# Two blocks of a network on one core: both FFNs' second products in seven block products instead of eight

## The reference

```python
def conv_ffn(h, p):                       # first block; D_FF = 2816
    a, b = jnp.split(h @ p["ffn_w_up"], 2, axis=-1)
    a = short_conv(a, p["ffn_conv_w"], p["ffn_conv_b"])
    return (jax.nn.gelu(a, approximate=False) * b) @ p["ffn_w_down"]

def conv_glu(x, w_up, conv_w, conv_b, w_down):   # second block
    hid = conv3(x @ w_up) + conv_b        # causal, per feature
    gate, up = hid[..., :D_FF], hid[..., D_FF:]
    return (jax.nn.silu(gate) * up) @ w_down
...
    x = x + g_f * conv_ffn(...)           # first block
    x = x + conv_glu(...)                 # second block
```

## Time and profile before

| | us |
|---|---|
| runs of the kernel, median of 3 (lowest to highest) | 3330.58 (3327.54 to 3332.19) |
| the profiled execution, its own time | 3329.57 |
| its span in the trace | 3327.7 |
| TensorE busy (matmuls) | 3179.3 (96%) |
| VectorE busy | 2189.8 (66%) |
| ScalarE busy | 1247.1 (37%) |
| POOL busy | 858.4 (26%) |
| mean granted clock of TensorE | 0.979 |
| down, first FFN | about 1487.5 to 1729.7 |
| down, second FFN | about 3084.8 to 3324.4 |

### The profile page before, as it was taken

How to read it: one execution, slowest core, us unless ns; L and a number is a source line. 1 busy time by engine, 2 the same in 40 slices (tenths; PEclk the granted TensorE clock), 3 DMA queues, 4 the chain that set the end, 5 groups by cost and what they waited for, 6 DMA issues and landing times.

```text
span 3327.7 us, 37104 instructions
## 1 busy us (share of the span) xinstructions
PE 3179.3 (96%) x14586; PEld 2477.6 (74%) x14586; DVE 2189.8 (66%) x2724; ACT 1247.1 (37%) x1912; POOL 858.4 (26%) x858
## 2 busy tenths in 40 slices
...
GB/s 227 158 136 118 146 202 45 45 9 247 223 145 162 100 84 83 83 124 170 156 120 115 102 127 184 177 107 39 38 72 117 155 83 83 89 83 84 198 133 123
DMA packets 110518, 406.82 MB, mean 122 GB/s; under 512 B 14376, under 2 KB 17000, under 8 KB 105866
## 3 DMA queue, kind: packets, MB, share of 16 engines
...
## 4 chain that ended last, share of the span: by engine, by line
PE 65%; DVE 8%; ACT 2%; issue 2%; POOL 1%; DMA 0%; ACTq 0%; DVEq 0%; POOLq 0%
PE PS L395 20%; PE PS L397 20%; PE PS L396 20%; PE PS L3112 2%; PE PS L3151 2%; PE PS L3134 1%; DVE HL L351 1%; POOL Sc L3360 1%; DVE E L3286 1%; ACT HL L333 0%; PE PS L2774 0%; DVE HT L1903 0%; DVE H L3412 0%; DVE HTf L1786 0%; DVE H L2498 0%
## 5 line engine op out<-in xcount | busy, mean ns | idle before, releaser
L395 PE MATMUL PS<-H,HL 128*128 128x512 f32 x1920 | 759.6, 396 | 15.2 <-DVE H L3412 7.3
L397 PE MATMUL PS<-H,HL 128*128 128x512 f32 x1920 | 751.1, 391 | 0.0
L396 PE MATMUL PS<-H,HL 128*128 128x512 f32 x1920 | 751.0, 391 | 0.0
L351 DVE TENSOR_TENSOR HL<-RAW,HL 128x512 fp32r<-128x512 f32 (+1 forms) x407 | 438.1, 1077 | 414.9 <-ACT HL L333 405.3
L333 ACT ACTIVATE HL<-RAW 128x512 fp32r<-128x512 f32 (+1 forms) x407 | 337.6, 830 | 921.6 <-PE PS L397 859.3
L395 PEld LDWEIGHTS PS<-H,HL 128*128 128x128 f32 x1920 | 362.6, 189 | 104.8 <-issue 19.7
L396 PEld LDWEIGHTS PS<-H,HL 128*128 128x128 f32 x1920 | 362.7, 189 | 76.5 <-issue 2.6
L397 PEld LDWEIGHTS PS<-H,HL 128*128 128x128 f32 x1920 | 362.4, 189 | 76.3
L395 PE MATMUL PS<-HT,HL 128*128 128x512 f32 x720 | 282.6, 393 | 17.8 <-DVE rows L2225 15.7
L396 PE MATMUL PS<-HT,HL 128*128 128x512 f32 x720 | 281.8, 391 | 0.0
L397 PE MATMUL PS<-HT,HL 128*128 128x512 f32 x720 | 281.4, 391 | 0.0
...
## 6 DMA issues: line engine op xcount, KB each, us to landing
RAW<-in_w_up SPq DMA_DIRECT2D x100, 512.0 KB, 3.6
RAW<-in_w_down SPq DMA_DIRECT2D x88, 512.0 KB, 3.6
RAW<-in_w_proj SPq DMA_DIRECT2D x48, 512.0 KB, 3.7
scr_hid<-hidr POOLq DMA_DIRECT2D x36, 512.0 KB, 2.9
...
RAW<-in_w_wmodr SPq DMA_DIRECT2D x32, 512.0 KB, 4.3
HL<-in_w_dfwd POOLq DMA_DIRECT2D x16, 1024.0 KB, 7.1
HL<-in_w_dinv POOLq DMA_DIRECT2D x16, 1024.0 KB, 5.3
```

Of the source, the lines that this page charges most:

```text
L351: e.tensor_tensor(lo, part_source(k, j, x)[0], hi.bitcast(F32), ALU.subtract).then_inc(*k.low.mark(j, x))
L395: e.matmul(out, lh, rh, start=first, stop=False)
L396: e.matmul(out, lh, rl, start=False, stop=False)
L397: return e.matmul(out, ll, rh, start=False, stop=last)
```

## The change

The hidden rows of a *pair* of blocks (2p, 2p+1) and the two halves of the tokens form a 2 x 2 matrix of blocks, and so do the two blocks' weights and the two halves of the 1024 output features. Their product takes seven block products of 128 x 128 x 512 by four banks instead of eight. There are 11 pairs (`PAIRS`; the two kept pairs come first) and seven phases (`PHASES`): m1, m2, m6, m7, m5, m4, m3. All 11 pairs of a phase follow one another, twelve matmuls each: 77 steps.

- The sums of results are not formed on VectorE. A phase goes on adding in the banks that the earlier one used: m1, m6, m5, m3 in banks 0 to 3, m2, m7, m4 in banks 4 to 7 (only m1, m2 and m7 begin anew). After each phase its four banks are added to the quarter of the residual that they then belong to (`ADDED`). Every addition waits for the residual's four loads, as before.
- All 18 stored blocks are loaded once, in twelve larger loads, into room that the up stage has left (`load_place`: `Hf`, `HTf`, `rows`, `cv2`) and stay there. POOL issues them ahead of the residual's loads; those into `rows` and `cv2` wait for the last hidden block.
- VectorE forms the sums of rows in place (`hidden_sum`, 44 an FFN, when: `T_AT`) and the sums of weights eight steps ahead (`weight_sum`): for m6 two operations per pair (out of a "sum" unit and half a "spare" unit in `RAW`), whose result `s2` is kept, and from it m5's and m3's by one each; m7's by one out of a "difference" unit. m1, m2 and m4 use weights as they are.
- Weights are loaded in units of two half blocks ("halves"), and for m6 in 6 spare and 11 sum units, for m7 in 11 difference units. A sum or spare unit's buffer comes free when its sum is done.
- Rows are split four steps ahead, into four places (`hs3` is new), weights six steps ahead by halves.
- The residual's features are complete in another order (`SETTLED`), and the norm between the FFNs follows it; two of its weight units are split earlier, and the last four additions stand behind them.

Core of the diff:

```diff
+PHASES = ["m1", "m2", "m6", "m7", "m5", "m4", "m3"]
+PAIRS = [9, 10] + list(range(9))
+NP = len(PAIRS)
+GROUPS = [[i for i in (g, g + 1) if i < NP] for g in range(0, NP, 2)]
...
-        for _ in range(2):
-            units(down, DOWN)
+        for x in PHASES:
+            for g, steps in enumerate(GROUPS):
+                if x != "m7":
+                    out.append((down, (x, g), "spare" if x == "m6" else "halves"))
+                if x in ("m6", "m7"):
+                    out.extend((down, (x, i), "sum" if x == "m6" else "difference") for i in steps)
...
+def down_source(k, name, i, kind):
+    x, n = i
+    w = k.A["w_" + name]
+    if kind == "difference":
+        return w[2 * PAIRS[n]]
+    if kind == "sum":
+        return w[2 * PAIRS[n]:2 * PAIRS[n] + 2, :, 512:1024].rearrange("t k n -> k t n")
+    p, m = PAIRS[GROUPS[n][0]], len(GROUPS[n])
+    f, h = {"m1": (0, 0), "m2": (1, 0), "m6": (0, 0), "m5": (0, 0), "m4": (1, 1), "m3": (1, 0)}[x]
+    return w.rearrange("(p two) k n -> two k p n", two=2)[f][:, p:p + m, blk(h, 512)]
...
+            elif before in ("halves", "difference"):
+                e.wait_ge(*k.low.at(b, down_parts(k.sched[b][1], before)[-1]))
+            elif before in ("spare", "sum"):
+                x, n = k.sched[b][1]
+                e.wait_ge(*ffn_of(k, b).s.dve.at("ws", 2 * NP + (GROUPS[n][-1] if before == "spare" else n)))
             else:
                 e.wait_ge(*k.low.at(b, "m4"))
-        e.dma_start(k.RAW[:, k.slot[j], :], k.A["w_" + name][i]).then_inc(*k.raw[k.slot[j]].mark(j))
+        if kind in DOWN_KINDS:
+            src = down_source(k, name, i, kind)
+            if kind == "difference":
+                to = k.RAW[:, k.slot[j], :]
+            else:
+                n = 2 if kind == "sum" else len(GROUPS[i[1]])
+                to = k.RAW[:, k.slot[j], 0:512 * n].rearrange("p (t n) -> p t n", t=n)
+        else:
+            src, to = k.A["w_" + name][i], k.RAW[:, k.slot[j], :]
+        e.dma_start(to, src).then_inc(*k.raw[k.slot[j]].mark(j))
...
+N_HS = 4
...
+SUMMED = ("m6", "m7", "m5", "m3")
+ADDED = {"m1": (0, range(0, 4)), "m2": (0, range(0, 4)), "m6": (0, range(4, 8)), "m7": (1, range(4, 8)), "m5": (1, range(4, 8)),
+         "m4": (0, range(4, 8)), "m3": (1, range(0, 4))}
+SETTLED = [list(range(8)), [4, 5, 6, 7, 0, 1, 2, 3]]
+MID_BANKS = [4, 5, 6, 7, 0, 1, 2, 3]
+T_AT = {}
+for _x, _i, _n in ([("t3", 0, 1), ("t3", 1, 2), ("t2", 0, 2), ("t2", 1, 3)] + [(x, i, 2 + i) for i in range(2, NP) for x in ("t3", "t2")]
+                   + [("t1", i, 30 + i) for i in range(NP)] + [("t4", i, 47 + i) for i in range(NP)]):
+    T_AT.setdefault(_n, []).append((_x, _i))
...
+def down_bank(x, d):
+    return d if x in ("m1", "m6", "m5", "m3") else 4 + d
...
+LOADS = [(f, h, p, n) for f, h in ((0, 0), (1, 0), (1, 1), (0, 1)) for p, n in (((0, 4), (4, 2), (6, 3)) if (f, h) == (0, 1) else ((0, 4), (4, 4), (8, 1)))]
...
+def load_place(k, m):
+    return [k.Hf[:, 0, 0:4, 0:512], k.Hf[:, 1, 0:4, 0:512], k.HTf[:, 0, 0, 0:1, :],
+            k.Hf[:, 0, 0:4, 512:1024], k.Hf[:, 1, 0:4, 512:1024], k.HTf[:, 0, 0, 1:2, :],
+            k.Hf[:, 0, 4:8, 0:512], k.Hf[:, 1, 4:8, 0:512], k.HTf[:, 0, 0, 2:3, :],
+            k.rows[:, :, :].rearrange("p a (b n) -> p (a b) n", n=512), k.cv2[:, :].rearrange("p (b n) -> p b n", n=512), k.HTf[:, 0, 1, 0:3, :]][m]
...
+def hidden_sum(k, e, F, t, i):
+    s = F.s
+    (b11, in11), (b12, in12) = hidden(k, F, 0, 0, i), hidden(k, F, 0, 1, i)
+    (b21, in21), (b22, in22) = hidden(k, F, 1, 0, i), hidden(k, F, 1, 1, i)
+    if t == "t3":
+        e.wait_ge(*in12)
+        e.wait_ge(*in22)
+        e.tensor_tensor(b12, b22, b12, ALU.subtract).then_inc(*s.dve.mark("t3", i))
...
+def weight_sum(k, e, F, n):
+    s, x, i = F.s, PHASES[n // NP], n % NP
+    if x not in SUMMED:
+        return
+    j, part = F.down_part[n]
+    u, h = k.RAW[:, k.slot[j], :], int(part[1])
+    e.wait_ge(*k.raw[k.slot[j]].at(j))
+    if x == "m6":
+        b = k.sched.index((k.sched[j][0], ("m6", i // 2), "spare"))
+        e.wait_ge(*k.raw[k.slot[b]].at(b))
+        e.tensor_tensor(u[:, 0:512], u[:, 0:512], u[:, 512:1024], ALU.add).then_inc(*s.dve.mark("ws1", n))
+        e.wait_ge(*s.dve.at("ws1", n))
+        if i == NP - 1:
+            e.wait_ge(*s.act.at("s1", NF - 1))
+        e.tensor_tensor(k.s2[i], u[:, 0:512], k.RAW[:, k.slot[b], blk(i % 2, 512)], ALU.subtract).then_inc(*s.dve.mark("ws", n))
+    elif x == "m7":
+        e.tensor_tensor(u[:, 0:512], u[:, 0:512], u[:, 512:1024], ALU.subtract).then_inc(*s.dve.mark("ws", n))
+    else:
+        a = u[:, blk(h, 512)]
+        e.wait_ge(*s.dve.at("ws", PHASES.index("m6") * NP + i))
+        if x == "m5":
+            e.tensor_tensor(a, k.s2[i], a, ALU.add).then_inc(*s.dve.mark("ws", n))
+        else:
+            e.tensor_tensor(a, a, k.s2[i], ALU.subtract).then_inc(*s.dve.mark("ws", n))
...
 def pe_down(k, e, F, free):
     s, PS = F.s, k.PS
     held = []
-    for n in range(2 * NF):
-        hf, first, last = n // NF, n % NF == 0, n % NF == NF - 1
-        j, uh, ul = take(k, e, F.down, DOWN[n % NF])
-        hs = k.hs2[:, n % 3]
+    for n, (j, part) in enumerate(F.down_part):
+        x, i = PHASES[n // NP], n % NP
+        w = take_part(k, e, j, part)
         e.wait_ge(*s.dve.at("hs", n))
-        if n >= 2 * NF - 2:
...
+        if n >= 7 * NP - 2:
+            held.append((j, part, w, hs))
             continue
-        for d, dt in enumerate(ORDER):
...
+        for d in range(4):
+            b = down_bank(x, d)
+            if i == 0:
+                for y in free[b]:
+                    e.wait_ge(*y)
+            y = mm3(e, PS[:, b, :], w[0][:, blk(d)], w[1][:, blk(d)], hs[:, 0, :], hs[:, 1, :], i == 0 and x in ("m1", "m2", "m7"), i == NP - 1, True)
+            if i == NP - 1:
+                free[b] = [s.dve.at("x", x, d)]
+                if d < 3:
+                    y.then_inc(*s.pe.mark("down", x, d))
+        y.then_inc(*s.pe.mark("hs", n))
+        k.used[j, part] = s.pe.at("hs", n)
+        if n == 7 * NP - 4 and not F.second:
             free = mid_sum(k, e, F, free, 0)
...
 def act_down(k, e, F):
-    for n in range(2 * NF):
-        if n + 2 < 2 * NF:
-            hs_high(k, e, F, n + 2)
-        if not F.second and NF <= n < NF + 8:
-            mid_squares(k, e, F, 0, n - NF)
-        if n < 2 * NF - 2:
-            split_high(k, e, F.first_down + n + 3)
-
-
-def left_down(k, e, F, hf, d):
-
-    s, PS, dt = F.s, k.PS, ORDER[d]
-    x = res(k, dt, hf)
-    e.wait_ge(*down_sum(F, hf, d))
+    hs_high(k, e, F, 2)
+    hs_high(k, e, F, 3)
+    for n in range(7 * NP - 4):
+        if n + N_HS < 7 * NP:
+            hs_high(k, e, F, n + N_HS)
+        if n + 6 < 7 * NP:
+            split_high_by(k, e, F.down_part[n])
+        if not F.second and n >= 57 and n % 2 and n < 65:
+            mid_squares(k, e, F, 0, (n - 57) // 2)
...
+def left_down(k, e, F, x, d):
+    s, b = F.s, down_bank(x, d)
+    h, dts = ADDED[x]
+    dt = dts[d]
+    r = res(k, dt, h)
+    e.wait_ge(*down_sum(F, x, d))
     e.wait_ge(*k.in_res2.at(F.s, 1, 1))
+    before = {"m2": "m1", "m5": "m7", "m4": "m6"}.get(x)
+    if before:
+        e.wait_ge(*s.dve.at("x", before, d))
...
 def dve_down(k, e, F):
-    for n in range(2 * NF):
-        split_low(k, e, F.first_down + n + 2 if n < 2 * NF - 1 else F.first_down + 2 * NF)
-        if n == NF - 1:
-            for d in range(8):
-                left_down(k, e, F, 0, d)
-        if n + 2 < 2 * NF:
-            hs_low(k, e, F, n + 2)
-        if not F.second and NF + 2 <= n < NF + 9:
-            mid_add(k, e, F, 0, n - NF - 1)
+    hs_low(k, e, F, 2)
+    hs_low(k, e, F, 3)
+    for n in range(7 * NP - 4):
+        if n + N_HS < 7 * NP:
+            hs_low(k, e, F, n + N_HS)
+        if n % NP == 0 and n:
+            for d in range(4):
+                left_down(k, e, F, PHASES[n // NP - 1], d)
+        if n + 6 < 7 * NP:
+            split_low_by(k, e, F.down_part[n])
+        for t, i in T_AT.get(n, []):
+            hidden_sum(k, e, F, t, i)
+        if n + 8 < 7 * NP:
+            weight_sum(k, e, F, n + 8)
...
 def pool_down(k, e, F):
     s = F.s
-    for m in range(N_HALF):
+    for m in (0, 1, 2):
+        load_hidden(k, e, F, m)
+    for m in (6, 9, 7, 10, 8, 11):
+        load_hidden(k, e, F, m)
+    for m in (3, 4, 5):
         load_hidden(k, e, F, m)
     for hf in range(2):
         for a in range(2):
             e.wait_ge(*s.pe.at("m4", NF - 1))
             e.dma_start(k.HTf[:, 2 - hf, a], k.d_res[4 * a:4 * a + 4, :, blk(hf, 512)].rearrange("d p n -> p d n")).then_inc(*k.in_res2.mark(s, hf, a))
-    for m in range(N_HALF, len(LOADED)):
-        if m == len(LOADED) // 2 + N_HALF and not F.second:
-            mid_store(k, e, F, 0)
-        load_hidden(k, e, F, m)
...
```

More of the change, by code:

```diff
@@ L390, in take_part, with mm3 @@
     return part_slot(k, k.pieces.index[j, x])
-def mm3(e, out, lh, ll, rh, rl, first, last):
-    e.matmul(out, lh, rh, start=first, stop=False)
```

(44 more changed lines are left out.)

159 lines of the change are left out of this document (98 added, 61 removed).

## The result

| | median us | lowest to highest | runs |
|---|---|---|---|
| before | 3330.76 | 3327.54 to 3332.19 | 4 |
| after | 3311.23 | 3308.61 to 3312.38 | 4 |

The ratio is 0.9942, 95% interval 0.9924 to 0.9959: 19.5 us faster (14 to 25). The forecast was 3299 in 3278 to 3322, so the direction and the range held, and 12 us of the forecast gain of 32 did not come. The profiled execution took 3312.38 us, with a span of 3310.6 (before 3329.57 and 3327.7).

What follows compares the result with a forecast made beforehand. TensorE was taken to bound both second products. -59.9 + 2.7 + 7.7 + 18.0 + 1.0 - 1.5 = -32.0 us against 3329.57 gave 3297.6, as a median 3299 us, range 3278 to 3322.

Steps and rivals of the forecast that it cites:

- 1. Matmuls removed: Both FFNs' second products: 264 fewer matmuls at 0.2267 us each, -59.9 us if TensorE never waits.
- 2. VectorE's load at nothing: Second products: 281 VectorE operations per FFN cost 171 to 200 us beside TensorE's 209, so nothing charged for throughput.
- VectorE is the bound: Rival: VectorE's operations run at full length, 0.683 us and more, four costing 2.8 us; 3307 us, chance 0.12.
- 3. Start: Start of each second product: step 2's rows are split behind the last hidden block; +0.6 and +2.1, +2.7 us together.
- 4. Residual: First additions wait for the residual's loads, queued behind the hidden rows, delaying step 16 by 3.9 us; +7.7 us for both FFNs.
- the 392 of the sum: DMA rate in GB/s when full, used to time the residual's landing: 10.2 MB at 392 less 96 for weights, 34.5 us.
- 5. Weights of m6: Product m6: buffers released in threes make two steps last 7.4 us against TensorE's 5.44; 9.0 per FFN, +18.0 us.
- weight landings decide: Rival: in m6 each group's first weight load lands in 7.3 us, not 3.6; 3336 us, slower, chance 0.12.
- 6. Clock: Matmuls run at half clock after pauses at steps 2 and 16, mostly hidden in later waits; +1.0 us (0 to +7).
- The turn between the FFNs: Between the FFNs: half of the last additions come after the first two H blocks TensorE waits for; -1.5 us.
- fed all through: Rival: weights come early enough and the residual's rows get more DMA, so TensorE is never starved; 3272 us, chance 0.13.

Runs made afterwards that it cites:

- the two versions that let TensorE run: Changed kernel with hidden loads reordered, rows 2 and 3 split earlier, and m6's spare weights in separate buffers (3268.51 us) or its loads swapped in order (3268.93 us).

## Why the prediction held, and where it was off

**1. Matmuls removed: right.** 264 fewer, and the two versions that let TensorE run return all of 59.9 us (59.7 and 61.9 by the medians).

**2. VectorE's load at nothing: right.** It waits 22.3 us in 1490:1600, for the residual and m6's weights. The rival "VectorE is the bound" needed it busy without a gap. The Trainium skill, VectorE: DVE Perf Modes, "The DRAIN you can't avoid", by whose rule the prediction had four operations take 2.8 us, adds in the same section that an operation that is not held starts earlier. The trace agrees with that addition: 0.60 us from start to start of operations of 0.68 us, in the changed kernel and in every version of it.

**3. Start: 4.0 for 2.7.** First FFN: wait 1.57 (forecast 1.5), step 2 at 1492.86. Second: 4.34 (forecast 3). There VectorE, whose weight splits now come two for one, reached the last evacuation later than TensorE's end, and then waited 0.63 us for a ScalarE copy that I had counted as earlier.

**4. Residual: 8.9 for 7.7, right in mechanism and place.** L2518's first addition started at 1530.27 (forecast 1530.4), behind an idle 8.5 us (forecast 11), and step 16 at 1535.67 (forecast 1535.6). The second FFN's pause there was only 1.57 us, since TensorE came later by its longer pause at step 2 and by 2.4 us of slow matmuls behind it, which are part of this stretch's 4.2: one lateness can't be charged twice. The windows say how full DMA was, answering:

```profile
1500.00:1510.00 10.00, 10.00 (x46) 8.27 (x45) 8.82 (x14) 3.96 (x7) 0.96 (x2) 1.00 1.03 387
1510.00:1520.00 10.00, 10.00 (x46) 8.29 (x45) 9.56 (x16) 4.12 (x8) 0.00 (x0) 1.00 1.04 386
```

387 and 386 GB/s, near the 392 of the sum. The Trainium skill's 358 GB/s (DMA: Bandwidth & Descriptors, "Where 436 GB/s comes from"), which it works out as half of what two cores share, is passed here, where one core runs.

**5. Weights of m6: 25.5 for 18.0. This is the step that failed, in size.** "Two steps cost: landing 3.6, sum 1.3, two splits 1.2, sum 1.3 = 7.4 us" was the right cycle with each piece too small. Measured in the first FFN: 7.92, 8.03, 8.25 and 8.92. From the release to the sum that needs a load it is 3.97, 4.08, 4.30 and 4.98, and not 3.6 (the earlier trace rows has the median of a stage that asks for one load every 5.4 us). The three loads of a group are asked for at once, and the median landing is longer there (issued in 1552.9:1554.5) than behind m6, where they come one at a time (1590:1620); the page has the median of all, 3.9:

```profile
RAW<-in_w_down SPq DMA_DIRECT2D x3, 512.0 KB, 4.9
...
RAW<-in_w_down SPq DMA_DIRECT2D x11, 512.0 KB, 3.6
...
RAW<-in_w_down SPq DMA_DIRECT2D x104, 512.0 KB, 3.9
```

The longest, 4.98, comes after POOL's stores of the residual; that they made it so was not tested. VectorE's part is 3.95 and not 3.8, since a dependent operation starts 0.72 later. The four additions at step 22 fell into a wait, as forecast: 0.46 us of it was left. One more piece was missing: rows 21 were to be split 14.7 us after step 16's start, but that is when the split began (1550.37), and a step starts 0.83 us after its split begins (1558.29 and 1559.12 for step 23). In the first FFN the cycles make 3.5 of the 4.4 us beyond 9.0, and this 0.8; the second FFN is 3.1 beyond.

The rival "weight landings decide" (6.8 us and more) did not come.

**6. Clock: +1.0 charged, nothing of its own found.** After pauses of 4.3 and 4.4 us matmuls ran at half pace and, with the restart, 2.6 and 3.0 us were lost. Behind the second:

```profile
1535.70:1541.00 5.30, 5.30 (x13) 4.15 (x14) 5.16 (x9) 0.00 (x0) 0.00 (x0) 0.50 0.30 100
```

In the changed kernel all of it was absorbed: the wait at step 21 never came in the first FFN, the second FFN's 2.4 us stood in the place of a longer wait at step 16, and the slow matmuls inside m6 (1.7 us behind the pause at step 27, in the second FFN at step 21 too) lie in cycles whose length the weights set. Behind the last pause, at step 29, none followed.

The turn between the FFNs, forecast -1.5, is -0.6. Up to 1765 us it had gained 3.5: TensorE waited 5.2 us for H blocks instead of 6.1, and fewer slow matmuls followed. But then it waited 3.62 us for VectorE's copy at L2789, where before it had waited 2.28 for ScalarE's, and with slow matmuls behind it this took 2.9 back.

The sum was thus off by 10.5 us: 7.5 in part 5, 1.3 in part 3, 1.2 in part 4, 1.5 in the turn and the last additions, less the 1.0 charged for the clock; the rival "fed all through", 3272, is what the mended versions reach.
